# Gate GEMMs of a streaming encoder layer as block products of pairs, with the later jobs moved into the sliding-window stage and the rotation moved to VectorE

## The chip, the cores and the metric

The kernel runs on one NeuronCore of one Trainium2 chip. The metric is the device time of one execution in microseconds (us). The engines are TensorE (PE), VectorE (DVE), ScalarE (ACT), GpSimd (POOL) and SyncE (SP, here a DMA queue). All arithmetic is fp32. A product of two fp32 matrices is made of three passes: each operand is split into a high part that TensorE takes exactly (`hi`, written by ACT) and the rest (`lo`, written by DVE), and TensorE computes `lo*hi + hi*lo + hi*hi`.

## The reference, cut to what matters

One layer for 640 token rows (a prompt of 512 frames, and 8 streams of 16 new frames), model width 1024:

```
h      = rmsnorm(x) * g_pre_mix
z      = h @ w_in            # q latent 384 | kv latent 256 | rope key 32 | swa q 512, k 128, v 128 | gate logits 2048
q      = (rmsnorm(z_q) * g_q) @ w_uq,   ckv = rmsnorm(z_kv) * g_kv       # q's and k's last columns are rotated (rope)
o_mla  = latent attention, 8 heads, chunk-causal; the streams also read 128 cached frames
o_swa  = sliding window of 128 frames, 8 query and 2 key heads, with sinks
m      = sum_b sigmoid(gate_b) * (o_b @ w_branch[b])
x      = x + rmsnorm(m @ w_out)
x      = x + rmsnorm((silu(h2 @ w_gate) * (h2 @ w_up)) @ w_down),  h2 = rmsnorm(x) * g
```

The gate logits are a product of 640 x 1024 with 1024 x 2048. They are needed only when the branches are mixed, late in the kernel, and wait for it in a DRAM scratch.

## The kernel before, in words

The program is written out by hand: each engine has one instruction stream, and counting semaphores tie them. There is no planner. In order of time the stages are:

1. **Norm and input projection** (to 96.2 us): `tall` (L1207 on) makes the 1440 mixer columns of `z` in three chunks of 480 columns.
2. **First gates** (to 152.5): 8 slots of 128 gate columns. `wide` (L1184) runs 8 row blocks of the contraction by 2 token halves by 3 passes, 48 matmuls of 128x128 by 320 columns per slot. While it runs, ACT squares `z`, DVE normalises it, and POOL applies the rotation to all five token tiles at once (`rope_out`, L529 to L536), and then sends the new rows out (24 DMAs).
3. **Turns** (to 160.2): jobs of three kinds per token tile (`qlat`, `ckv`, `qs`) transpose `z` on PE; ACT and DVE copy the banks out.
4. **Query up-projection** (to 175.8): 10 jobs `uq`, each 9 matmuls of 384 columns.
5. **Sliding window** (to 253.9): 8 chunks of 64 frames. Per chunk PE makes `chunk_scores` (L1433), one gate slot with `chunk_values` of the previous chunk (L1458) in its middle, and `chunk_turn` (L1443). DVE takes the maximum (L1820), ACT the exponentials (L963), DVE divides (L1830), PE turns the result, ACT copies it (L973).
6. **Remaining jobs** (to 282.9): `kt` (keys from the latent), `q` (turning q), `cache` (turning the caches), `wuk`, `v`, `qabs`. They use four PSUM banks in turn, and PE waits with job j until job j-4 is copied out. The last `chunk_values` stands among them.
7. **Attention units**, then branches and mixing, output projection, the gate/up stage of the FFN, and the down projection.

A job's copies run on ACT where its number is odd and on DVE where it is even (`job_engine`). Every engine takes its instructions in order, so a copy that is written behind the exponentials of a chunk waits for them.

The FFN's gate/up stage of this kernel already works as block products of pairs: two weight columns of 128 and two token halves give a 2x2 block product over a contraction split in two, made with 7 products of 12 matmuls for 8. It is the same recipe that the change takes to the gates, so its rows serve below as measured prices of the new instructions: `L1952` a difference of two weight blocks on DVE, `L1036` a high part on ACT, `L1898` a low part on DVE, and 320-column reads of a bank (`L1095`, `L2018`).

Lines of the profile that the prediction uses: L1180 to L1182 (the three passes), L1306 `q`, L1310 to L1312 `cache`, L1317 `wuk`, L1328 `qabs`, L1332 `kt`, L1336 `v`, L802 (POOL clears `probs_m` behind a wait for all of `cv_done`).

## Time and profile before

| | before |
|---|---|
| median of 3 runs | 902.55 us (902.31 to 903.01) |
| the profiled execution's own time | 903.12 us |
| its span in the trace, granted TensorE clock | 901.3 us, 0.998 |
| PE, PEld busy | 885.1 us (98%), 804.0 us (89%) |
| DVE, ACT, POOL busy | 491.9, 385.4, 75.7 us |
| chain that ended last | PE 90%, DVE 5%, ACT 4%, issue 1% |
| matmuls, HBM traffic | 5513, 102 GB/s over the span |

The span runs from the first to the last instruction of the trace; 1.8 us of the execution lie around it. A row of busy time merges overlapping instructions: a 320-column matmul is shown with 309 ns, though one starts every 147 ns, because their ends overlap. The chain of waits shows the time that each piece adds.

### The profile page before, as it was taken

How to read it: one execution, taken by the hardware profiler on the slowest of the kernel's cores; microseconds unless marked ns; L12 is line 12 of the kernel's file. 1: busy time of each engine (PE TensorE's matmuls, PEld its weight loads, DVE VectorE, ACT ScalarE, POOL GpSimd, SP SyncE). 2: the span in 40 equal slices, each digit the busy share in tenths (PEclk: the TensorE clock that was granted, in tenths of full speed). 3: DMA queues.
4: the chain of work that ended last, by engine and by line, in shares of the span. 5: the costliest groups of instructions: out<-in, count | busy, mean ns of one | idle time of the engine just before them, and what ended most of it. 6: DMA issues, size and time to landing. Idle time of an engine off the chain costs nothing.

```text
span 901.3 us, 13817 instructions
## 1 busy us (share of the span) xinstructions
PE 885.1 (98%) x5513; PEld 804.0 (89%) x5513; DVE 491.9 (55%) x758; ACT 385.4 (43%) x769; POOL 75.7 (8%) x73
## 2 busy tenths in 40 slices
PE   8999999999999998999999999999999999999997
PEld 7888999999976877998789999999999998888886
DVE  5523532433354565564779877777777774343124
ACT  5211422335453555452666545444445443332112
POOL 0300197140030000000000000000000000000000
PEclk9999999999999999999999999999999999999999
DMA  7623245153330001654612233332233326222202
GB/s 271 176 78 93 69 128 179 57 158 92 100 71 1 2 1 36 205 181 181 193 72 81 83 93 95 94 87 76 73 94 94 94 84 242 72 72 93 71 24 117
DMA packets 101599, 91.97 MB, mean 102 GB/s; under 512 B 8496, under 2 KB 85312, under 8 KB 101392
## 3 DMA queue, kind: packets, MB, share of 16 engines
q1 hardware_dynamic: 95216, 86.19, 30.9%
q10 hardware_dynamic: 5424, 2.99, 1.1%
q0 software_dynamic: 896, 1.92, 0.7%
q8 instruction: 44, 0.72, 0.3%
q14 instruction: 19, 0.16, 0.1%
HBM read 79.60 MB, written 12.40 MB: 102 GB/s over the span
## 4 chain that ended last, share of the span: by engine, by line
PE 90%; DVE 5%; ACT 4%; issue 1%; DMA 0%; DVEq 0%; POOL 0%; ACTq 0%; POOLq 0%
PE ps L1180 26%; PE ps L1181 25%; PE ps L1182 25%; PE ps L1362 2%; PE ps L1411 1%; PE ps L1373 1%; PE ps L1235 1%; PE ps L1458 1%; PE ps L1332 1%; PE ps L1405 1%; PE ps L1336 1%; ACT probs L897 1%; PE ps L1433 1%; PE ps L1443 1%; DVE nm_c L1735 1%
## 5 line engine op out<-in xcount | busy, mean ns | idle before, releaser
L1671 DVE TENSOR_TENSOR wlo<-raw,whi 128x1024 fp32r<-128x1024 f32 x59 | 79.0, 1342 | 206.0 <-ACT whi L824 198.5
L824 ACT ACTIVATE whi<-raw 128x1024 fp32r<-128x1024 f32 x59 | 62.1, 1056 | 179.3 <-PE ps L1182 167.6
L1180 PE MATMUL ps<-h_hi,wlo 128*128 128x320 f32 x288 | 90.7, 315 | 0.0
L1182 PE MATMUL ps<-h_hi,whi 128*128 128x320 f32 x288 | 89.0, 309 | 0.0
L1181 PE MATMUL ps<-h_lo,whi 128*128 128x320 f32 x288 | 88.9, 309 | 0.0
L1180 PE MATMUL ps<-sc_hi,t_lo 128*128 128x320 f32 x252 | 77.9, 309 | 0.9 <-DVE t_lo L1898 0.9
L1036 ACT ACTIVATE t_hi<-wd 128x512 fp32r<-128x512 f32 x84 | 52.8, 629 | 60.3 <-DVE wd L1952 55.9
L1182 PE MATMUL ps<-sc_hi,t_hi 128*128 128x320 f32 x252 | 77.8, 309 | 0.0
L1181 PE MATMUL ps<-sc_lo,t_hi 128*128 128x320 f32 x252 | 77.8, 309 | 0.0
L1180 PE MATMUL ps<-whi,gu_lo 128*128 128x512 f32 x190 | 74.0, 390 | 0.2 <-DVE gu_lo L2022 0.2
L1181 PE MATMUL ps<-wlo,gu_hi 128*128 128x512 f32 x190 | 73.9, 389 | 0.0
L1182 PE MATMUL ps<-whi,gu_hi 128*128 128x512 f32 x190 | 73.9, 389 | 0.0
L1898 DVE TENSOR_TENSOR t_lo<-wd,t_hi 128x512 fp32r<-128x512 f32 x84 | 57.6, 686 | 2.0
L1180 PEld LDWEIGHTS ps<-h_hi,wlo 128*128 128x128 f32 x288 | 54.0, 188 | 2.8 <-issue 2.5
L1181 PEld LDWEIGHTS ps<-h_lo,whi 128*128 128x128 f32 x288 | 54.1, 188 | 0.0
L1182 PEld LDWEIGHTS ps<-h_hi,whi 128*128 128x128 f32 x288 | 54.1, 188 | 0.0
L1181 PE MATMUL ps<-h_lo,b_hi 128*128 128x320 f32 x168 | 51.8, 308 | 0.0
L1182 PE MATMUL ps<-h_hi,b_hi 128*128 128x320 f32 x168 | 51.7, 307 | 0.0
L1180 PE MATMUL ps<-h_hi,b_lo 128*128 128x320 f32 x168 | 51.5, 307 | 0.0
L1180 PEld LDWEIGHTS ps<-sc_hi,t_lo 128*128 128x128 f32 x252 | 47.3, 188 | 1.2 <-DVE t_lo L1898 1.2
L1182 PEld LDWEIGHTS ps<-sc_hi,t_hi 128*128 128x128 f32 x252 | 47.3, 188 | 0.0
L1181 PEld LDWEIGHTS ps<-sc_lo,t_hi 128*128 128x128 f32 x252 | 47.3, 188 | 0.0
(308 smaller groups left out, 2143.9 us busy)
## 6 DMA issues: line engine op xcount, KB each, us to landing
raw<-in_w_gate_up SPq DMA_DIRECT2D x44, 512.0 KB, 3.8
raw<-in_w_down SPq DMA_DIRECT2D x22, 512.0 KB, 3.7
raw<-in_w_in SPq DMA_DIRECT2D x16, 512.0 KB, 4.1
raw<-in_w_in SPq DMA_DIRECT2D x12, 480.0 KB, 4.8
gates_scratch<-gate_s SPq DMA_DIRECT2D x16, 320.0 KB, 2.4
gate_r<-gates_scratch SPq DMA_DIRECT2D x8, 640.0 KB, 4.4
raw<-in_w_branch SPq DMA_DIRECT2D x8, 512.0 KB, 5.3
raw<-in_w_out SPq DMA_DIRECT2D x8, 512.0 KB, 6.0
```

The lines of the kernel that those rows point to most:

```text
L824: act.activation(whi[:, r % 2, :] if to is None else to, raw[:, r, :], ACT.Copy).then_inc(w_hi, 1)
L897: act.activation((probs if of_prompt else probs_m)[:, 2 * slot + c, 0:nk], ps[:, b0 + c, 0:nk], ACT.Exp, bias=nm_c[:, col:col + 1], accum_ ...
L1036: act.activation(op_parts(kind, p)[0][:], op_source(kind, p), ACT.Copy).then_inc(op_hi_rdy, 1)
L1180: pe.matmul(out, left[1], right[0], start=first, stop=False, skip_group_check=not own_group)
L1181: pe.matmul(out, left[0], right[1], start=False, stop=False, skip_group_check=not own_group)
L1182: return pe.matmul(out, left[0], right[0], start=False, stop=last, skip_group_check=not own_group)
L1235: pe.transpose(ps[:, 7, 0:P], ident[:], ident[:])
L1332: ins = pe.matmul(bank[:, :], w_uk[:, ct, 2 * n:2 * n + 2, :], ckv_T[:, ct, 0:SEQ], start=(ct == 0), stop=(ct == 1))
L1336: ins = pe.matmul(bank[:, :], ckv_T[:, ct, c], w_uv[:, ct, :, :], start=(ct == 0), stop=(ct == 1))
L1362: ins = pe.matmul(out[:, 0:nk], q_T[:, h, a * P:(a + 1) * P], k_T[:, h, 0:nk], start=True, stop=True)
L1671: dve.tensor_tensor(lo[:, place, :], raw[:, r, :], hi[:, place, :].bitcast(F32), ALU.subtract).then_inc(w_lo, 1)
L1898: dve.tensor_tensor(lo[:], op_source(kind, p), hi[:].bitcast(F32), ALU.subtract).then_inc(op_lo_rdy, 1)
```

## The change

What it does:

- **Gates as one block of pairs.** The 16 gate columns become 8 pairs. Each pair takes 7 products of 12 matmuls (`gate_product`), 56 products in all, in one unbroken stage behind the input projection. Four of the seven weight operands of a pair are differences of blocks (`gate_difference`, DVE); ACT and DVE split each operand to hi and lo (512 columns each). Four sums of blocks of `h` are made once on DVE during the input projection (`h_add`, `hs_raw`, `part_sum_lo`; ACT `part_sum_hi`). ACT and DVE combine the products (`gate_read`), four reads on ACT and three on DVE per pair.
- **Rotation on VectorE.** `rope_products` (4 instructions) and `rope_sums` (6) of a token tile stand behind products 2, 7, ... and 4, 9, ... of the gate stage; `z_normalise` (10) behind products 13, 15, ... 31 and the key's rotation behind 34 and 36. The squares are on ACT behind products 1 to 10.
- **Jobs in the sliding-window stage.** `uq` 0 and 1 stay ahead of it; all other jobs stand inside the chunks (`CHUNK_JOBS`: a part between scores and the previous chunk's values, a part before the turn, a part behind it). They have two banks (`job_bank`), so PE waits with job j until job j-2 is copied out. Behind chunk 1, ACT and DVE split the two first branch weights. `chunk_values` of the last chunk is now the last of the stage.
- The loads of `w_ukv` move from ACT's queue at the start to SP's queue behind the gates; the cache loads wait for `uq` 8 and 9. POOL's rotation of q starts once `uq` 9 is copied out, and `cache` jobs wait for it.

The order of instructions on PE at the end of the sliding-window stage of the kernel before (`L1443` turn of the last chunk, `L1332` `kt`, `L1458` values, `L1306` `q`, `L1310` to `L1312` one `cache` job):

```order
L1443 MATMUL ps<-ident,probs_s 128x128 x8
L1332 MATMUL ps<-ckv_T,w_uk 128x512 x4
L1458 MATMUL ps<-pt_s,v_s 64x128 x8
L1332 MATMUL ps<-ckv_T,w_uk 128x512 x4
L1306 MATMUL ps<-ident,q_t 96x128 x40
L1310 MATMUL ps<-ident,c_ckv 128x128 x2
L1311 MATMUL ps<-ident,c_k 128x128
L1312 MATMUL ps<-ident,c_kpe 32x128
```

And on PE in chunk 4 of the changed kernel (`L1585` scores, `L1467` the four `wuk` jobs, `L1609` values of chunk 3, then the first of eight `cache` jobs; its turn, `L1596`, follows the eighth):

```order
L1585 MATMUL ps<-ks_T,qs_T 128x192 x4
L1467 MATMUL ps<-ident,w_uk 64x128 x16
L1609 MATMUL ps<-pt_s,v_s 64x128 x8
L1460 MATMUL ps<-ident,c_ckv 128x128 x2
L1461 MATMUL ps<-ident,c_k 128x128
L1462 MATMUL ps<-ident,c_kpe 32x128
```

The `cache`, `wuk` and `q` jobs stood one behind another with no softmax beside them; now they stand between the scores and the turn of a chunk. The last rows of that stage on PE in the changed kernel (`L1478` `qabs` 3, `L1488` `v` 2, the turn of chunk 7, `v` 3, its values):

```order
L1478 MATMUL ps<-q_Ts,wuk_T 128x128 x4
L1488 MATMUL ps<-w_uv,ckv_T 128x512 x2
L1596 MATMUL ps<-ident,probs_s 128x128 x8
L1488 MATMUL ps<-w_uv,ckv_T 128x512 x2
L1609 MATMUL ps<-pt_s,v_s 64x128 x8
```

In the kernel before, `kt`, `q` and the other jobs followed the values of chunk 7; now the attention units follow at once.

DVE in the gate stage of the kernel before (between the last copy of `z` and the first job):

```order
L1712 COPY z<-ps 128x480 x5
L1671 TENSOR_TENSOR wlo<-raw,whi 128x1024
L1723 RECIPROCAL r_z<-sd_z 128x5
L1726 SCALAR_TENSOR_TENSOR z<-z,r_z,gq_b 128x384 x5
L1723 RECIPROCAL r_z<-sd_z 128x5
L1726 SCALAR_TENSOR_TENSOR z<-z,r_z,gkv_b 128x256 x5
L1671 TENSOR_TENSOR wlo<-raw,whi 128x1024 x7
```

DVE around product 8 of the changed kernel (`L1938` and `L1934` reads of a bank, `L1917` a difference, `L1903` a low part, `L1956` and `L1957` the sums of the rotation of tile 1; its four products of 320 columns, `L1948`, stand just ahead):

```order
L1938 TENSOR_TENSOR g_out_102<-ps,g_u_0_98 128x320
L1917 TENSOR_TENSOR wd_g<-raw,wd_g 128x512
L1903 TENSOR_TENSOR g_m_lo<-raw,g_m_hi 128x512
L1903 TENSOR_TENSOR g_m_lo<-wd_g,g_m_hi 128x512
L1956 TENSOR_TENSOR z<-rope_a,rope_b 128x4x32
L1957 TENSOR_TENSOR z<-rope_c,rope_d 128x4x32
L1956 TENSOR_TENSOR z<-rope_a,rope_b 128x4x32
L1957 TENSOR_TENSOR z<-rope_c,rope_d 128x4x32
L1956 TENSOR_TENSOR z<-rope_a,rope_b 128x2x32
L1957 TENSOR_TENSOR z<-rope_c,rope_d 128x2x32
L1917 TENSOR_TENSOR wd_g<-raw 128x512
L1903 TENSOR_TENSOR g_m_lo<-raw,g_m_hi 128x512
```

Eight splits of 1024 columns have become 56 low parts and 32 differences of 512 columns, 24 reads, and the rotation between them.

The diff, cut to its core:

```diff
-JOBS = (
-    [(kind, t) for t in range(TILES) for kind in ("qlat", "ckv", "qs")]
-    + [("uq", n) for n in range(2 * TILES)]
-    + [("kt", n) for n in range(4)] + [("q", n) for n in range(2 * TILES)] + [("cache", b) for b in range(STREAMS)]
-    + [("wuk", n) for n in range(4)] + [("v", 0), ("v", 1)] + [("qabs", n) for n in range(4)] + [("v", 2), ("v", 3)]
-)
-JOBS1 = 5 * TILES
+TURNS = [(kind, t) for t in range(TILES) for kind in ("qlat", "ckv", "qs")]
+JOBS1 = len(TURNS)
+
+
+
+AHEAD = [("uq", 0), ("uq", 1)]
+CHUNK_JOBS = [
+    ([("uq", 2)], [("uq", 3), ("uq", 4)], []),
+    ([("uq", 5)], [("uq", 6), ("uq", 7)], []),
+    ([("uq", 8)], [("uq", 9), ("kt", 0)], []),
+    ([("kt", 1)], [("kt", 2), ("kt", 3)], []),
+    ([("wuk", n) for n in range(4)], [("cache", b) for b in range(STREAMS)], []),
+    ([("q", n) for n in range(4)], [("q", n) for n in range(4, 10)], []),
+    ([("v", 0)], [("v", 1), ("qabs", 0)], []),
+    ([("qabs", 1), ("qabs", 2)], [("qabs", 3), ("v", 2)], [("v", 3)]),
+]
+JOBS = TURNS + AHEAD + [job for chunk in CHUNK_JOBS for part in chunk for job in part]
...
-    return 4 + (j + 3) % 4 if j < JOBS1 else (j - JOBS1) % 4
+    return 4 + (j + 1) % 4 if j < JOBS1 else (j - JOBS1) % 2
...
+GATE_PAIRS = 8
+GATE_PRODUCTS = [("m1", 0), ("m2", 0)]
+for p in range(GATE_PAIRS - 1):
+    GATE_PRODUCTS += [("m5", p), ("m6", p), ("m1", p + 1), ("m7", p), ("m2", p + 1), ("m4", p), ("m3", p)]
+GATE_PRODUCTS += [(kind, GATE_PAIRS - 1) for kind in ("m5", "m6", "m7", "m4", "m3")]
+NG = len(GATE_PRODUCTS)
+GATE_BANKS = [(7, 0, 1), (2, 3, 4)]
...
+            def store_gates(p):
+                sp.wait_ge(g_c11, p + 1)
+                sp.wait_ge(g_c21, p + 1)
+                sp.dma_start(gates_dram[2 * p], g_out_s[p % 2][0][:]).then_inc(g_st[p % 2][0], 16)
+                sp.wait_ge(g_c22, p + 1)
+                sp.wait_ge(g_c12, p + 1)
+                sp.dma_start(gates_dram[2 * p + 1], g_out_s[p % 2][1][:]).then_inc(g_st[p % 2][1], 16)
...
+            sp.wait_ge(gp_used, NG)
+            for k in range(2):
+                sp.dma_start(w_uk[:, k], w_ukv[0, k * P:(k + 1) * P, :, 0:NOPE]).then_inc(wukv_in, 16)
+                sp.dma_start(w_uv[:, k], w_ukv[0, k * P:(k + 1) * P, :, NOPE:NOPE + VDIM]).then_inc(wukv_in, 16)
+            sp.dma_start(q_T[96:128], mask_q_dram.unsqueeze(1).to_broadcast([32, HEADS, SEQ])).then_inc(mask_in, 16)
+            sp.dma_start(k_T[96:128], mask_k_dram.unsqueeze(1).to_broadcast([32, HEADS, SEQ])).then_inc(mask_in, 16)
+            job_emptied(sp, job_index("uq", 8))
+            job_emptied(sp, job_index("uq", 9))
...
+            pool.wait_ge(gp_used, NG)
+            pool.tensor_copy(v_s[:], z[:, :, C_VS:MIX_COLS]).then_inc(v_s_rdy, 1)
+            job_emptied(pool, job_index("uq", 8))
+            job_emptied(pool, job_index("uq", 9))
...
+            def gate_split_hi(m):
+                kind, p = GATE_PRODUCTS[m]
+                if kind in DIFFERENCES:
+                    act.wait_ge(gp_diff, gate_difference_count(kind, p))
+                else:
+                    s = gate_slots(p)[kind == "m3"]
+                    act.wait_ge(w_raw[s % 4], 16 * (s // 4 + 1))
+                if p:
+                    act.wait_ge(gp_used, gate_count(kind, p - 1))
+                act.activation(gp_hi[kind][:], gate_source(kind, p), ACT.Copy).then_inc(gp_hi_rdy, 1)
...
+            for n in range(NG):
+                gate_read(n)
+                if n + LEAD + 1 < NG:
+                    gate_split_hi(n + LEAD + 1)
+                if 1 <= n <= 2 * TILES:
+                    z_square(n - 1)
...
+            def gate_product(n):
+                kind, p = GATE_PRODUCTS[n]
+                b_p, b_q, b_r = GATE_BANKS[p % 2]
+                bank = {"m2": b_q, "m5": b_r, "m3": b_r}.get(kind, b_p)
+                first = kind in ("m1", "m2", "m5")
+                left = {"m1": (0, 0), "m2": (4, 0), "m4": (4, HALF)}.get(kind)
+                i = {"m5": 0, "m6": 1, "m7": 2, "m3": 3}.get(kind)
+                pe.wait_ge(gp_lo_rdy, n + 1)
+                if kind == "m1":
+                    pe.wait_ge(g_c21, p - 1) if p >= 2 else pe.wait_ge(bank_empty, 10 + 5 * p)
+                elif kind == "m2" and p >= 2:
+                    pe.wait_ge(g_c11, p - 1)
+                elif kind == "m5" and p >= 2:
+                    pe.wait_ge(g_c12, p - 1)
+                elif kind == "m6":
+                    pe.wait_ge(g_u1_rdy, p + 1)
+                elif kind == "m7":
+                    pe.wait_ge(g_u2_rdy, p + 1)
+                elif kind == "m4":
+                    pe.wait_ge(g_u3_rdy, p + 1)
+                elif kind == "m3":
+                    pe.wait_ge(g_c22, p + 1)
+                if p == 0 and i is not None:
+                    pe.wait_ge(hs_lo_rdy, i + 1)
+                for k in range(4):
+                    w = slice(k * P, (k + 1) * P)
+                    if left is None:
+                        right = (hs_hi[:, i, k, :], hs_lo[:, i, k, :])
+                    else:
+                        cols = slice(left[1], left[1] + HALF)
+                        right = (h_hi[:, left[0] + k, cols], h_lo[:, left[0] + k, cols])
+                    ins = mm3(ps[:, bank, 0:HALF], (gp_hi[kind][:, w], gp_lo[kind][:, w]), right, first and k == 0, k == 3,
+                              first)
+                ins.then_inc(gp_used, 1)
...
+                elif j >= JOBS1 + 2:
+                    job_emptied(pe, j - 2)
...
             for c in range(NCH):
                 chunk_scores(c)
-                pe.wait_ge(w_lo, G1 + c + 1)
-                pe.wait_ge(g_out, 8 + c)
-                wide(c % 2, h_hi, h_lo, (0, 1), 0, 4, KD)
+                for j in chunk_jobs(c, 0):
+                    job(j)
                 if c:
                     chunk_values(c - 1)
-                wide(c % 2, h_hi, h_lo, (0, 1), 4, KD, KD).then_inc(w_used, 1)
+                for j in chunk_jobs(c, 1):
+                    job(j)
                 chunk_turn(c)
-            for j in range(JOBS1, len(JOBS)):
-
-                if j == JOBS1:
-                    pe.wait_ge(g_out, 16)
-                elif j == JOBS1 + 2:
-                    chunk_values(NCH - 1)
-                job(j)
+                for j in chunk_jobs(c, 2):
+                    job(j)
+            chunk_values(NCH - 1)
...
+            def h_add(half, part):
+
+                own = slice(4 * part, 4 * part + 4), slice(HALF * half, HALF * half + HALF)
+                dve.tensor_tensor(h_part[half, part][:], h_hi[:, own[0], own[1]].bitcast(F32),
+                                  h_lo[:, own[0], own[1]].bitcast(F32), ALU.add).then_inc(hs_part, 1)
+
+            def part_sum_lo(i):
+                dve.wait_ge(hs_hi_rdy, i + 1)
+                dve.tensor_tensor(hs_lo[:, i], hs_raw[:, i], hs_hi[:, i].bitcast(F32), ALU.subtract).then_inc(hs_lo_rdy, 1)
...
+            def gate_difference(kind, p):
+                gate, up = (s % 4 for s in gate_slots(p))
+                of = {"m5": (raw[:, up, 0:512], raw[:, gate, 0:512]),
+                      "m6": (raw[:, up, 512:1024], gate_source("m5", p)),
+                      "m7": (raw[:, up, 512:1024], raw[:, up, 0:512]),
+                      "m4": (raw[:, gate, 512:1024], gate_source("m6", p))}[kind]
+                if kind == "m5":
+                    for s in gate_slots(p):
+                        dve.wait_ge(w_raw[s % 4], 16 * (s // 4 + 1))
+                else:
+                    dve.wait_ge(gp_diff, gate_difference_count(kind, p) - 1)
+                dve.tensor_tensor(gate_source(kind, p), of[0], of[1], ALU.subtract).then_inc(gp_diff, 1)
+
...
+            def rope_products(t):
+                qk = z[:, t, C_QS:C_VS].rearrange("p (h d) -> p h d", d=HD)
+                cos_b = cos_t[:, t, :].unsqueeze(1).to_broadcast([P, 10, 32])
+                sin_b = sin_t[:, t, :].unsqueeze(1).to_broadcast([P, 10, 32])
+                if t:
+                    dve.wait_ge(z_rot, ROPE_STEPS * t)
+                for to, x, factor in ((rope_a, qk[:, :, 0:32], cos_b), (rope_b, qk[:, :, 32:64], sin_b),
+                                      (rope_c, qk[:, :, 32:64], cos_b), (rope_d, qk[:, :, 0:32], sin_b)):
+                    dve.tensor_tensor(to[:], x, factor, ALU.mult).then_inc(z_rot, 1)
+
+            def rope_sums(t):
+
+                pairs = z[:, t, C_QS:C_KS].rearrange("p (i g d) -> p i g d", i=4, g=2)
+                keys = z[:, t, C_KS:C_VS].rearrange("p (h d) -> p h d", d=HD)
+                dve.wait_ge(z_rot, ROPE_STEPS * t + 4)
+                for heads, to in ((slice(0, 4), pairs[:, :, 0, :]), (slice(4, 8), pairs[:, :, 1, :]), (slice(8, 10), keys)):
+                    dve.tensor_tensor(to[:, :, 0:32], rope_a[:, heads], rope_b[:, heads], ALU.subtract).then_inc(z_rot, 1)
+                    dve.tensor_tensor(to[:, :, 32:64], rope_c[:, heads], rope_d[:, heads], ALU.add).then_inc(z_rot, 1)
...
+            for n in range(NG):
+                gate_read(n)
+                if n + LEAD + 1 < NG and GATE_PRODUCTS[n + LEAD + 1][0] in DIFFERENCES:
+                    gate_difference(*GATE_PRODUCTS[n + LEAD + 1])
+                if n + LEAD < NG:
+                    gate_split_lo(n + LEAD)
+                if n < 5 * TILES and n % 5 == 2:
+                    rope_products(n // 5)
+                elif n < 5 * TILES and n % 5 == 4:
+                    rope_sums(n // 5)
+                if 13 <= n < 13 + 4 * TILES and n % 2:
+                    z_normalise((n - 13) // 2)
+                elif n == 34:
+                    key_rope_products()
+                elif n == 36:
+                    key_rope_sums()
...
+                for j in chunk_jobs(c, 0):
+                    job(j)
                 chunk_normalise(c)
                 if c:
                     chunk_out(c - 1)
-                after_slot(G1, 0, c)
+                for part in (1, 2):
+                    for j in chunk_jobs(c, part):
+                        job(j)
+                if c == 1:
+                    split_lo(BRC + 1, 0)
+                    split_lo(BRC + 2, 1)
```

## Rows read from the trace of the kernel before

**Rows 1.** Windows: us, then PE, PEld, DVE, ACT, POOL busy (x), clock, DMA share, GB/s

```profile
50.00:100.00 50.00, 50.00 (x241) 43.86 (x240) 16.61 (x18) 10.88 (x17) 0.72 (x1) 1.00 0.28 73
...
96.20:152.50 56.30, 56.30 (x385) 56.28 (x384) 19.64 (x22) 18.52 (x37) 43.65 (x43) 1.00 0.47 133
152.50:160.23 7.73, 7.39 (x58) 5.90 (x57) 5.84 (x17) 4.40 (x9) 0.85 (x1) 1.00 0.15 61
160.23:175.84 15.61, 15.61 (x93) 15.36 (x91) 5.93 (x16) 4.11 (x7) 0.00 (x0) 1.00 0.06 22
175.84:253.85 78.01, 78.01 (x601) 72.48 (x601) 26.66 (x38) 35.74 (x103) 14.00 (x12) 1.00 0.39 113
253.85:282.93 29.08, 29.08 (x171) 19.86 (x171) 15.50 (x29) 13.69 (x30) 9.17 (x10) 1.00 0.24 56
```

**Rows 2.** Timeline of the FFN's gate/up stage: start, us, instruction [idle before <-releaser]

```profile
602.13 0.49 DVE L2018 TENSOR_TENSOR gu_f<-c,u 128x320 f32<-128x320 f32 x1
602.54 0.69 DVE L1952 TENSOR_TENSOR wd<-raw,wd 128x512 f32<-128x512 f32 x1
603.14 0.68 DVE L1898 TENSOR_TENSOR b_lo<-raw,b_hi 128x512 fp32r<-128x512 f32 x1
603.26 0.64 ACT L1036 ACTIVATE t_hi<-wd 128x512 fp32r<-128x512 f32 x1 [2.53 <-DVE wd L1952]
...
605.06 0.44 ACT L1095 ACTIVATE u<-ps 128x320 f32<-128x320 f32 x1 [0.64 <-PE ps L1182]
```

**Rows 3.** Timeline of DVE, first gate stage: the normalising

```profile
103.95 2.74 DVE L1726 SCALAR_TENSOR_TENSOR z<-z,r_z,gq_b 128x384 f32<-128x384 f32 x5
```

**Rows 4.** Timeline of ACT around chunk 6 of the sliding window

```profile
234.26 1.08 ACT L973 ACTIVATE pt_s<-ps 128x512 f32<-128x512 f32 x2
...
236.52 0.42 ACT L963 ACTIVATE probs_s<-ps,nm_c 128x193 f32<-128x193 f32 x1 [1.19 <-DVE nm_c L1820]
```

**Rows 5.** The same chunk's rows of DVE

```profile
235.53 0.95 DVE L1820 TENSOR_REDUCE nm_c<-ps 128x4 f32<-128x772 f32 x1
238.28 0.18 DVE L1828 RECIPROCAL inv_c<-sum_c 128x4 f32<-128x4 f32 x1 [1.79 <-ACT probs_s L963]
238.49 0.96 DVE L1830 TENSOR_TENSOR probs_s<-probs_s,inv_c 128x768 f32<-128x768 f32 x1
```

**Rows 6.** Costliest groups: splits of a 1024-column slot, busy us, mean ns

```profile
L1671 DVE TENSOR_TENSOR wlo<-raw,whi 128x1024 fp32r<-128x1024 f32 x59 | 79.0, 1342 | 206.0 <-ACT whi L824 198.5
L824 ACT ACTIVATE whi<-raw 128x1024 fp32r<-128x1024 f32 x59 | 62.1, 1056 | 179.3 <-PE ps L1182 167.6
```

**Rows 7.** Chain of waits, last chunk and the jobs behind it: start, us, piece

```profile
243.67 0.85 PE ps L1433 x8
...
252.98 0.87 PE ps L1443 x8
253.85 3.68 PE ps L1332 x8
257.54 1.02 PE ps L1458 x16
...
262.19 4.55 PE ps L1306 x40
...
270.23 1.87 PE ps L1317 x16
...
275.54 3.77 PE ps L1328 x32
```

**Rows 8.** Timeline of DVE: copies of a `q` job and of a `cache` job

```profile
265.47 0.69 DVE L1784 TENSOR_SCALAR q_T<-ps 96x512 f32<-96x512 f32 x1 [0.19 <-PE ps L1306]
...
269.11 0.42 DVE L1786 COPY ckv_Ta<-ps 128x256 f32<-128x256 f32 x1
...
269.75 0.28 DVE L1786 COPY kpe_Ta<-ps 32x128 f32<-32x128 f32 x1
```

**Rows 9.** Timeline of POOL, end of the jobs stage

```profile
259.50 0.95 POOL L802 MEMSET probs_m<- 128x1024 f32 x1
```

435 lines of the change are left out of this document (271 added, 164 removed).

## The prediction

> **What bounds the kernel now.** I read three views. The windows by stage come first [rows 1]: from 96.2 us to 282.9 us PE is busy for 186.4 of 186.7 us at clock 1.00, while DVE has 73.6 and ACT 76.5 (sums over the last five rows). So in the whole stretch that the change rewrites PE is the bound, and what PE issues less is gained in full, as long as nobody makes it wait. The chain of waits [rows 7] confirms it: the pieces follow each other without a gap and carry PE's name. The timelines [rows 2 to 5, 8] then give prices of what DVE and ACT must do between two PE pieces, which decides whether PE stays unbroken. Before, every softmax chunk had a gate slot of 7 us as cover; that cover is what the change spends.
>
> **What PE saves.** The first gate window has 384 matmuls in 56.3 us, 147 ns each [rows 1]. Both gate stages are 768 matmuls (112.6 us); 56 products of 12 are 672 (98.5 us): 14.1 us less. A second, smaller gain: the sliding-window window takes 78.0 us [rows 1]; its gate slots are 56.3, and scores, turns and values at 0.85, 0.87 and 1.02 us [rows 7], with the two first, shorter chunks at about two thirds, come to 18.7. The 3.0 us left I put down to the change between softmax pieces and gate matmuls, some fifteen times 0.2; only `uq` jobs keep such changes, five of them, so 2.0 us go. The turns (7.7 us), `uq` (15.6) and the other jobs (29.1) stay as they are. PE's own work falls from 186.7 to 170.6 us.
>
> **What is hidden.** DVE makes twelve block sums or parts of `h` of 1280 columns in the input projection, 1.7 us each by the 1.34 us for 1024 [rows 6], some 20 us over 40; DVE is busy for 16.6 of 50 us there [rows 1] and the pieces stand between splits that have to wait anyway. I cost it at nothing; were it late, PE would wait for the weights of the projection. POOL's work behind the gates is 14.0 + 9.2 us [rows 1]; it starts when `uq` 9 is copied, with some 50 us left: nothing. The 24 stores on POOL's queue start behind product 36, 20 products before the end, and the loads of weights have the same pattern as in the FFN's stage, which shows no wait for them: nothing.
>
> **What DVE costs in the gate stage.** Per pair 11 instructions of 512 columns and 3 of 320. Start to start these take 0.60 us (602.54 to 603.14) and 0.41 us (602.13 to 602.54) [rows 2], so 1.12 us per product against PE's 1.76. The rotation of a tile is 4 instructions of 320 columns (1.64), and 6 of 128 and 64 columns, which the trace of before does not show. The step from 512 to 320 is 1 ns a column, which gives 0.22 and 0.15; with the wait for the products of 0.1 a tile costs 2.9 us. The bounds of a 128-column piece are 0.15 (as a 64-column one) and 0.29 (the whole 0.49 of a 320-column row less the columns), 2.6 to 3.3 us a tile. I take 2.9, by the row nearest to it. A normalising instruction is 0.55 for 384 columns [rows 3], 0.42 estimated for 256. DVE comes to product 1 at about 101.1 us, since the last copies of `z` and five splits stand ahead. To the end of product 25's share that is 25 x 1.12 + 5 x 2.9 + 4.1 (seven normalising, two reciprocals) = 46.6 us, so 147.7; PE would end product 25 at 141.9. What bites is not the low part, which has a lead of five products, but ACT's order: the read behind product 26, for which product 28 waits, stands behind a high part that waits for DVE's difference of that same share. Difference done at 146.8, high part 0.64, read 0.44 [rows 2]: 147.9, where product 28 would start at 145.4. That is 2.5 us, and with the hand-overs between I take 3.0. From product 33 on DVE has only its 1.12 per product and catches up, which gives nothing back. The last pair has no other pair's products between: m7 and m4 each wait for a read of 0.44 plus hand-over, 1.0 us together.
>
> One rule of the Trainium skill speaks against the price per instruction. On DVE two rows of 0.69 and 0.68 us stand 0.60 apart [rows 2]. The page VectorE: DVE Perf Modes, section The DRAIN you can't avoid, says that the next operation does not start before the pipe is empty; by that the distance would be the full length of a row. The trace of the FFN does not bear this out for independent instructions. What it would give is a rival below.
>
> **What two banks and the missing cover cost in the window stage.** I walk each chunk from its first score. A softmax takes scores 0.85, maximum 0.95, exponentials 1.76 (236.52 to DVE's 238.28), division 1.17, so PE can turn 4.8 us after the first score [rows 4, 5]; PE has 5.3 us and more of its own to do from the first score to the turn in every chunk, so alone this costs nothing. Four places do cost:
> - Chunk 2. ACT first copies chunk 1's turn (0.7), then two splits of 1.06; DVE's low parts (1.34 each [rows 6]) stand ahead of its maximum and end at 4.5, the maximum at 5.4, exponentials 7.2, division 8.3. PE's own work to the turn is 0.85 + 1.56 + 0.59 + 1.56 + 1.84 = 6.4: 1.9 us.
> - Chunk 4. `wuk` 3 needs the bank of `wuk` 1, whose copy on ACT stands behind the exponentials: 4.2 instead of 2.3. After the values (5.7) come eight `cache` jobs of 0.44 (266.74 to 270.23 [rows 7]), each with 0.92 of copies [rows 8]. With four banks the copies of the two engines overlapped PE's work; with two, a pair costs 0.44 + 0.92 + hand-overs, 1.5 us instead of 0.9. The turn can start at 11.4, own work is 7.2: 4.2 us.
> - Chunk 5. The same with ten `q` jobs (0.46 each [rows 7], copies 0.69 [rows 8]): turn at 9.5, own work 6.4: 3.1 us.
> - Chunk 7. `qabs` 3 waits for `qabs` 1 behind the exponentials: 0.5 us.
> At the end the values of chunk 7 have nothing behind them: POOL's 0.95 us for `probs_m` [rows 9], which waits for them, is now in PE's way, as are the two copies of the output: 1.1 us.
>
> **The sum.** 3.0 + 1.0 + 1.9 + 4.2 + 3.1 + 0.5 + 1.1 = 14.8 us of waits against 16.1 saved. 186.7 becomes 185.4. The profiled execution took 903.12 us (span 901.3 and 1.8 around it); less 1.3 is 901.8, and as that execution lies 0.57 above the median of the runs, 901.3 us.
>
> **The rivals.**
> - *DVE is the bound of the gate stage.* If an instruction holds DVE for its full row (0.69, 0.49, and 0.29 and 0.22 for the short ones), a product costs 1.29 and a tile 3.7 us; DVE ends product 25's share at 155.9 and product 28 starts 10.4 us late, 7.4 more: 909 us. It decides from where the five tiles and 25 products cost DVE more than 44 us. For it: each rotation starts with a wait on DVE's own last result, and strided halves of heads have no row here. Against it: 0.60 and 0.41 in the FFN. The skill's rule named above leads here. Slower. 0.20.
> - *The engines keep up better than my walk.* ACT's reads or short pieces of the rotation are cheaper and DVE has slack left, so that the gate stage flows (3.0) and chunk 2's splits fit in (1.9): 896.4, about 897 us. For it: each wait was worked out with hand-overs that the chain shows at only some 0.04 us. 0.20.
> - *Nothing waits*, and the full 16.1 us are gained: 886.5 us. Two banks against a copy of 0.92 speak against it. 0.04.
> - *A transfer is late.* The cache loads go out when `uq` 9 is copied, some 15 us before the first `cache` job; before, they had 78 us, so the trace does not bound their wait from above; `w_ukv` has some 28 us. At 5 us of waiting 906 us. 0.06.
>
> **How the numbers follow.** This kernel's measurement tells 0.2%, 1.8 us, from no change: faster is below 900.75, slower above 904.35. My forecast (0.50) spans 899 to 904.5, since each of the five larger waits may be off by a third: 0.15 of it is faster, 0.33 the same, 0.02 slower. Faster: 0.15 + 0.20 + 0.04 = 0.39. Same: 0.33. Slower: 0.20 + 0.06 + 0.02 = 0.28. The range 895 to 908 holds the forecast, the faster rival, the late transfer and the nearer half of DVE's rival (3.3 us a tile and some longer starts); left out are its far end and the full gain.
>
> **What would show it.** The gate stage from first to last of its matmuls lasts about 102.5 us, with PE whole for twenty products, gaps ahead of m4 of pairs 2 and 3 released by ACT's read `g_u3`, and two gaps of half a microsecond at the end. In the window stage PE waits at `kt` 0 and the turn of chunk 2, in the middle of `wuk`, between pairs of `cache` and `q` jobs, released by ACT's and DVE's copies, and hardly in chunks 0, 1, 3 and 6. Matmuls fall by 96. The forecast is wrong if PE waits from product 8 on at every m4 (DVE's rival), if it waits at the first `cache` job for a DMA, or if the input projection no longer ends at 96.2.

## The result, and the profile after

| kernel | median, us | executions | ratio to before (95% interval) |
|---|---|---|---|
| before | 902.50 | 6 (902.05 to 903.01) | |
| changed | 906.09 | 6 (904.20 to 907.10) | 1.0036 (1.0023 to 1.0049) |
| changed, second measurement, beside 27 executions of before (median 902.32) | 905.74 | 5 (905.03 to 907.49) | 1.0036 (1.0022 to 1.0050) |

The change makes the kernel slower by 0.36%, 3.6 us. The forecast was 901.3 us, with the kernel before and the changed one nearly level. The profiled execution of the changed kernel is its fastest, 904.20 us (span 902.4), so there are two things to explain: 2.9 us between forecast and that execution, and some 1.8 more in most of the others.

The page's line of busy times, and then windows of the changed kernel (us from the start, then PE, PEld, DVE, ACT, POOL busy, clock, DMA share, GB/s):

```profile
PE 873.0 (97%) x5417; PEld 787.8 (87%) x5417; DVE 561.4 (62%) x922; ACT 406.5 (45%) x829; POOL 45.4 (5%) x57
```

```profile
95.23:199.07 103.84, 99.71 (x674) 98.53 (x672) 82.37 (x177) 47.10 (x107) 12.52 (x24) 1.00 0.48 145
...
95.23:209.97 114.74, 110.21 (x747) 107.26 (x745) 91.16 (x205) 52.11 (x117) 13.23 (x25) 1.00 0.53 153
209.97:283.71 73.74, 64.83 (x457) 47.59 (x457) 36.61 (x65) 40.74 (x123) 21.67 (x18) 1.00 0.13 36
```

The 96 matmuls are gone (5513 to 5417 on PE). From the first gate matmul to the first of attention, the kernel before takes 186.56 us (96.21 to 282.77, PE busy for 186.22 of them); the changed one takes 114.74 + 73.74 = 188.48, and PE is busy for 175.04. So PE has 11 us less to do and waits 13 more. From the first attention matmul to the start of the last matmul of the kernel it is 612.61 us in the trace of before and 612.72 in that of the changed kernel. The start differs from execution to execution, not by the change: over the thirteen profiles of the changed kernel and its variants the gate stage begins between 94.86 and 96.24 us, and the 44 transposes that open the program take 6.4 to 7.9.

Every wait of the gate stage, in PE's timeline (start, us, instruction, [idle before <- who ended it]; `g_m_lo` is the low part of a weight operand, `g_u` a bank read by ACT):

```profile
134.09 0.38 PE L1293 MATMUL ps<-h_hi,g_m_lo 128*128 128x320 f32 x1 [1.38 <-ACT g_u L982]
...
148.05 0.38 PE L1293 MATMUL ps<-h_hi,g_m_lo 128*128 128x320 f32 x1 [1.40 <-ACT g_u L982]
...
192.86 0.39 PE L1293 MATMUL ps<-hs_hi,g_m_lo 128*128 128x320 f32 x1 [0.62 <-ACT g_u L978]
...
195.48 0.38 PE L1293 MATMUL ps<-h_hi,g_m_lo 128*128 128x320 f32 x1 [0.62 <-ACT g_u L982]
```

These are the m4 of pairs 2 and 3 and the last pair's m7 and m4, where the prediction put them. ACT's rows ahead of the first show the order that bites: the read `g_u` (L982) stands behind a high part that waited 2.38 us for DVE's difference.

```profile
132.99 0.63 ACT L964 ACTIVATE g_m_hi<-wd_g 128x512 fp32r<-128x512 f32 x1 [2.38 <-DVE wd_g L1917]
133.53 0.42 ACT L982 ACTIVATE g_u<-ps 128x320 f32<-128x320 f32 x1
```

DVE's timeline gives the prices of the short pieces for which [rows 2] had to stand in, read from start to start:

```profile
106.60 0.28 DVE L1956 TENSOR_TENSOR z<-rope_a,rope_b 128x128 f32<-128x128 f32 x1
106.80 0.28 DVE L1957 TENSOR_TENSOR z<-rope_c,rope_d 128x128 f32<-128x128 f32 x1
...
107.41 0.22 DVE L1956 TENSOR_TENSOR z<-rope_a,rope_b 128x64 f32<-128x64 f32 x1
107.54 0.22 DVE L1957 TENSOR_TENSOR z<-rope_c,rope_d 128x64 f32<-128x64 f32 x1
...
111.15 0.48 DVE L1948 TENSOR_TENSOR rope_a<-z,cos_t 128x320 f32<-128x320 f32 x1
111.55 0.48 DVE L1948 TENSOR_TENSOR rope_b<-z,sin_t 128x320 f32<-128x320 f32 x1
```

0.20 us for 128 columns, 0.13 for 64, 0.40 for 320: a tile costs 4 x 0.40 + 1.15 = 2.75 us (forecast 2.9). A full row each would set the two 128-column rows 0.28 apart; they are 0.20 apart. So the drain that the Trainium skill describes (VectorE: DVE Perf Modes, section The DRAIN you can't avoid) does not space these instructions; what the same section says of an operation that is not held, that it starts earlier, agrees with this 0.20.

The window stage, chunks 4 and 5, PE's rows with a wait (`L1467` is `wuk`, `L1460` `cache`, `L1455` `q`):

```profile
242.62 0.63 PE L1467 MATMUL ps<-ident,w_uk 128*64 128x128 f32 x4 [0.66 <-DVE wuk_T L2069]
244.25 0.63 PE L1467 MATMUL ps<-ident,w_uk 128*64 128x128 f32 x4 [1.00 <-ACT wuk_T L1061]
...
247.68 0.44 PE L1460 MATMUL ps<-ident,c_ckv 128*128 128x128 f32 x2 [0.75 <-DVE kpe_Ta L2069]
...
249.34 0.44 PE L1460 MATMUL ps<-ident,c_ckv 128*128 128x128 f32 x2 [0.57 <-DVE kpe_Ta L2069]
...
251.01 0.44 PE L1460 MATMUL ps<-ident,c_ckv 128*128 128x128 f32 x2 [0.57 <-DVE kpe_Ta L2069]
...
255.48 0.64 PE L1455 MATMUL ps<-ident,q_t 128*96 128x128 f32 x4 [0.65 <-DVE q_T L2067]
257.11 0.64 PE L1455 MATMUL ps<-ident,q_t 128*96 128x128 f32 x4 [0.99 <-ACT q_T L1061]
...
260.32 1.08 PE L1455 MATMUL ps<-ident,q_t 128*96 128x128 f32 x8 [0.53 <-DVE q_T L2067]
261.74 1.08 PE L1455 MATMUL ps<-ident,q_t 128*96 128x128 f32 x8 [0.34 <-DVE q_T L2067]
```

In the kernel before, the same jobs ran at four banks without a gap: `q` 4.55, `wuk` 1.87 us [rows 7], and the eight `cache` jobs 3.51, from the first of these rows of before to the second:

```profile
266.58 0.38 PE L1310 MATMUL ps<-ident,c_ckv 128*128 128x128 f32 x2
270.09 2.01 PE L1317 MATMUL ps<-ident,w_uk 128*64 128x128 f32 x16
```

In the changed kernel they take 6.10 us (245.84 to 251.94), of which the three rows above count 1.89 as idle. Chunk 2 waits at `kt` 0 and at its turn, `qabs` 3 waits 0.50, and attention begins behind POOL's clearing:

```profile
228.23 1.98 PE L1484 MATMUL ps<-ckv_T,w_uk 128*128 128x512 f32 x4 [0.46 <-DVE q_t L2069]
230.73 1.09 PE L1596 MATMUL ps<-ident,probs_s 128*128 128x128 f32 x8 [0.51 <-DVE probs_s L2113]
...
283.71 0.73 PE L1510 MATMUL ps<-ckv_Ta,qabs 128*128 128x144 f32 x4 [1.37 <-POOL probs_m L874]
```

### The profile page after: what moved, and what is told of

Same layout as the page of the kernel before. It is cut to its first block, busy times and chain, and to the rows that moved or that the text cites. A ratio compares the mean times of both kernels' runs of the same rounds, so it can differ in the third digit from the quotient of the medians.

```text
span 902.4 us, 13913 instructions
## 1 busy us (share of the span) xinstructions
PE 873.0 (97%) x5417; PEld 787.8 (87%) x5417; DVE 561.4 (62%) x922; ACT 406.5 (45%) x829; POOL 45.4 (5%) x57
## 3 DMA queue, kind: packets, MB, share of 16 engines
q0 software_dynamic: 896, 1.92, 0.6%
## 4 chain that ended last, share of the span: by engine, by line
PE 83%; DVE 8%; ACT 5%; DMA 2%; issue 1%; POOL 0%; SPq 0%; DVEq 0%; ACTq 0%; POOLq 0%
PE ps L1293 24%; PE ps L1294 24%; PE ps L1295 24%; PE ps L1514 2%; PE ps L1563 1%; PE ps L1525 1%; DMA raw<-in_w_out 1%; PE ps L1488 1%; PE ps L1557 1%; ACT probs_s L1075 1%; PE ps L1596 1%; ACT probs L1026 1%; DMA raw<-in_w_in 1%; DVE wlo L1818 1%; DVE nm_c L2018 1%
## 5 line engine op out<-in xcount | busy, mean ns | idle before, releaser
L1818 DVE TENSOR_TENSOR wlo<-raw,whi 128x1024 fp32r<-128x1024 f32 x43 | 52.4, 1224 | 119.7 <-ACT whi L896 112.2
L896 ACT ACTIVATE whi<-raw 128x1024 fp32r<-128x1024 f32 x43 | 45.2, 1059 | 162.3 <-PE ps L1295 160.1
L2182 DVE TENSOR_TENSOR b_lo<-raw,b_hi 128x512 fp32r<-128x512 f32 x63 | 43.1, 685 | 0.0
L1293 PEld LDWEIGHTS ps<-whi,gu_lo 128*128 128x128 f32 x190 | 35.7, 188 | 8.0 <-DVE gu_lo L2306 0.6
L964 ACT ACTIVATE g_m_hi<-wd_g 128x512 fp32r<-128x512 f32 x32 | 20.2, 630 | 49.1 <-DVE wd_g L1917 47.8
L1294 PEld LDWEIGHTS ps<-wlo,gu_hi 128*128 128x128 f32 x190 | 35.7, 188 | 7.4
L1295 PEld LDWEIGHTS ps<-whi,gu_hi 128*128 128x128 f32 x190 | 35.7, 188 | 7.3
L1293 PE MATMUL ps<-hs_hi,g_m_lo 128*128 128x320 f32 x128 | 39.6, 309 | 0.6 <-ACT g_u L978 0.6
```

The source lines that it names most:

```text
L896: act.activation(whi[:, r % 2, :] if to is None else to, raw[:, r, :], ACT.Copy).then_inc(w_hi, 1)
L964: act.activation(gp_hi[kind][:], gate_source(kind, p), ACT.Copy).then_inc(gp_hi_rdy, 1)
L1293: pe.matmul(out, left[1], right[0], start=first, stop=False, skip_group_check=not own_group)
L1294: pe.matmul(out, left[0], right[1], start=False, stop=False, skip_group_check=not own_group)
L1295: return pe.matmul(out, left[0], right[0], start=False, stop=last, skip_group_check=not own_group)
L1818: dve.tensor_tensor(lo[:, place, :], raw[:, r, :], hi[:, place, :].bitcast(F32), ALU.subtract).then_inc(w_lo, 1)
```

## The experiments

All were timed against the kernel before, in several executions each; "changed" is the kernel with the change, and "below the changed kernel" is counted from its second measurement, 905.74 us. That one stands beside g1_rope, s1_splits and w1_order; for the later experiments the kernel before had medians of 902.37 to 902.75 instead of 902.32, so their distance from the changed kernel is uncertain by some 0.5 us. Lengths of a stretch are read from one profiled execution each. The stretch named in them runs from the first gate matmul to attention, the window stage from the first window scores to attention.

**a0_again: the changed kernel, unaltered.** 

> The changed kernel once more, unaltered, timed against the kernel before. Its profiled execution took 904.2 us, five others 904.4 to 907.1, while six of the kernel before lay within 1.0 us. Theory 1 (waits of two engines that nearly tie, so the losses differ between executions; or a start that differs): median 905 to 906.5 again, about 0.3 to 0.4% above the kernel before, and a spread of 2 to 3 us. If the profiled execution is one of the slow ones, some stretch of its trace is longer than in the first trace, and that says where: in the start (0 to 95 us) if it is the start, in the gate stage (103.8 us long in the first trace) or the window stage (73.7 us from the first window scores to attention) if it is the new stages, after 290 us if it is neither. Rival: the first measurement was off and the median is within 0.2% of before.

Measured: 905.74 us. The first measurement was right, so the rival falls. The numbers of theory 1 hold, its causes do not: the profiled execution (906.06 us) has the same stretch to 0.01 us, 188.49, and starts it 0.22 us later. The rest of what it has more lies behind the stretch, in attention: 1.63 us from the first attention matmul to the last matmul. Windows of this execution, and then of the first one:

```profile
347.00:349.00 2.00, 1.75 (x10) 1.33 (x11) 0.97 (x2) 0.90 (x5) 0.00 (x0) 0.55 0.00 0
349.00:351.00 2.00, 2.00 (x10) 1.46 (x10) 0.58 (x1) 0.00 (x0) 0.00 (x0) 0.59 0.00 0
```

```profile
347.00:349.00 2.00, 1.98 (x16) 1.59 (x16) 0.96 (x3) 0.67 (x4) 0.00 (x0) 1.00 0.00 0
349.00:351.00 2.00, 1.49 (x12) 0.92 (x10) 1.70 (x6) 1.50 (x6) 0.00 (x0) 1.00 0.00 0
```

The third number from the right is the granted clock. For 3.4 us it is at 0.50 of full speed (1.2 of 2.4 GHz), and the same instructions take some 1.6 us longer. Ahead of the fall PE had waited 1.12, 0.21 and 0.45 us between short pieces; the execution without a fall has the same waits to 0.01 us.

The record of each execution has its mean granted clock. Of the eleven executions of the changed kernel in both measurements, five have a mean of 0.996 and took 905.74 to 907.49 us (on average 906.5), and six have 0.998 or 0.999 and took 904.20 to 906.48 (905.3). All 27 of the kernel before have 0.998 or more. The mean does not say where a fall lay: the end of most traces, where PE has no work left, is at half clock too, 2 to 3 us of it in the kernel before.

**g1_rope: rotation and normalising spread in DVE's order.** 

> Only VectorE's order in the gate stage changes: rotation of a tile every eighth product instead of every fifth, normalising every third instead of every second, the narrow keys at products 42 and 44. Same instructions. Theory 1 (VectorE's queue is late where rotation and normalising lie close together, which costs the two m4 waits of 1.4 us with their PEld idle): both waits go, gate stage 103.8 -> 100.8 to 101.3 us, time 2.5 to 3 us below the changed kernel (0.3%). Rival (the two waits come from ScalarE's own order, which reads bank u3 after the next splits): both waits stay and the time is within 0.5 us. Second rival: the stores of z go out 14 us later and the first up-projection waits for them: the gain is given back in one wait at the end of the turns.

```
-                if n < 5 * TILES and n % 5 == 2:          # sums: n % 5 == 4
+                if n < 8 * TILES and n % 8 == 2:          # sums: n % 8 == 5
-                if 13 <= n < 13 + 4 * TILES and n % 2:
+                if 13 <= n < 13 + 6 * TILES and n % 3 == 1:
```

Measured: 902.84 us (11 executions, 900.83 to 903.90), 2.9 below the changed kernel; ratio to before 1.0002 (0.9993 to 1.0011). Both m4 waits are gone, nothing new waits, and gates plus turns fall from 114.74 to

```profile
95.04:206.54 111.50, 109.73 (x746) 107.27 (x744) 90.87 (x205) 52.66 (x117) 13.24 (x25) 1.00 0.53 156
```

Theory 1 holds, and gives a second number: the waits were 1.38 + 1.40 = 2.78 us of idle time, and the stretch is 3.24 shorter. Each wait costs 0.23 us more than its row says, because the row counts only from the end of the matmul before, which is drawn 0.16 us into its follower (0.31 us long, the next one 0.15 later), and the matmul behind a wait is followed after 0.22 us (134.09 to 134.31) instead of 0.15.

**s1_splits: the branch-weight splits out of chunk 1.** 

> Only the two branch-weight splits move: ScalarE's and VectorE's halves from the end of chunk 1 to chunks 5 to 7 (ScalarE's behind its copies of the turned probabilities of chunks 5 and 6, VectorE's behind the maxima of chunks 6 and 7). Theory 1: the waits of chunk 2 (0.46 at the first key up-projection, 0.51 ahead of its turn) go, and chunks 6 and 7 hide the splits: time 1 to 1.9 us below the changed kernel. Rival: VectorE meets the splits again in chunks 6 and 7 and the turns there wait as long: same time within 0.4 us, with the wait moved.

```
 ACT   -  if c == 1: split_hi(0, ...); split_hi(1, ...)        # behind chunk_pt(c)
       +  if c in (5, 6): split_hi(c - 5, ...)
 DVE   -  if c == 1: split_lo(BRC + 1, 0); split_lo(BRC + 2, 1)
       +  if c in (6, 7): split_lo(BRC + c - 5, c - 6)         # behind chunk_max(c)
```

Measured: 903.77 us, 2.0 below. The window stage is 72.36 us long, 1.38 less, for two rows with 0.97 us of idle time together: 0.2 more for each wait again. Theory 1 holds.

**w1_order: the list of window jobs, first form.** 

> Only the list of jobs in the window stage changes: the query transposes, the w_uk transposes and the key up-projection alternate and stand at most two in a row, so that each copy out of a bank has another job or a part of a chunk beside it; the four cache jobs stay together. Theory 1 (with two banks, a transpose job of 0.9 us followed by its like waits for the copy before last, 0.5 to 1.0 us each): the waits between query jobs (0.65, 0.99, 0.53, 0.34) and at w_uk (0.66, 1.00) go, those between the cache jobs (three of 0.6) stay; stage 73.7 -> about 69.5 us, time 4 us below the changed kernel. Rival (what is lost is not these waits but the switch of TensorE between kinds of work, some 0.2 to 0.3 us each, of which this order has more): gain under 1.5 us, and the rows of busy PE become longer where waits go.

The list is shown shortened, from chunk 2 on: `uq 8` stands for `("uq", 8)`, `cache 0..7` for all eight.

```
-    ([uq 8], [uq 9, kt 0], []),              ([kt 1], [kt 2, kt 3], []),
-    ([wuk 0..3], [cache 0..7], []),          ([q 0..3], [q 4..9], []),
-    ([v 0], [v 1, qabs 0], []),              ([qabs 1, qabs 2], [qabs 3, v 2], [v 3])
+    ([uq 8], [uq 9, wuk 0], [wuk 1]),        ([kt 0], [wuk 2, kt 1], [wuk 3, kt 2]),
+    ([kt 3, q 0], [cache 0..7], [q 1]),      ([q 2, q 3], [v 0, q 4], [q 5, q 6]),
+    ([v 1, q 7], [q 8, q 9], []),            ([qabs 0, qabs 1], [qabs 2, qabs 3], [v 2, v 3])
```

(There are eight cache jobs, not four as the expectation says.) Measured: 902.62 us, 3.1 below. The waits between `q` jobs and between `wuk` jobs are gone. Chunk 2's first wait of 0.46 now stands ahead of `wuk` 0, its turn waits 1.87 us, and while the cache jobs waited (1.07, 0.60, 0.16 and 0.30 us), the clock fell:

```profile
250.00:253.00 3.00, 2.84 (x14) 2.17 (x13) 1.00 (x4) 0.82 (x3) 2.36 (x1) 0.50 0.00 0
```

The window stage is 71.16 us with that fall, an estimated 69.5 without it (less the 1.6 us that the fall cost in a0_again). Theory 1 holds, but this list can do better.

**w3_order: the list, second form, and nothing else.** 

> The changed kernel with only the list of window jobs altered, now with the eight cache jobs (0.5 us of TensorE each, copies of 1.0 us) set apart too, one or two beside a key or value up-projection of 1.8 us or a part of a chunk. The first reordering left the eight together: scores of chunk 0 to attention went from 73.7 to 71.2 us, with a clock fall of 1.7 us inside it. Theory 1 (waits with two banks, and each wait costs 0.2 us more than its idle row): the waits of the cache jobs go as well, this stretch is 68.5 to 69 us, and TensorE, never idle long, keeps its clock there: time 5 to 5.5 us below the changed kernel, 900.3 to 901. Rival (the copies are the bound: eight of 1.0 us and ten of 0.6 to 0.7 us beside the chunks' own work on two engines): waits move to the turns, stretch 71 us, time 902.5 as before.

```
+    ([uq 8], [uq 9, kt 0], [wuk 0]),         ([kt 2], [wuk 1, kt 1], [wuk 2]),
+    ([q 0, kt 3, cache 0], [cache 1, cache 2], [q 1, wuk 3]),
+    ([q 2, v 0, cache 3], [cache 4, q 3], [cache 5, q 4]),
+    ([cache 6, v 1, q 5], [q 6, q 7], [cache 7, q 8]),
+    ([v 2, q 9], [qabs 0, qabs 1], [qabs 2, qabs 3, v 3])
```

(With it, attention waits for `qabs` 3 too.) Measured: 897.44 us (897.11 to 898.00), 8.3 below the changed kernel, 0.9944 (0.9930 to 0.9958) of before. The window stage:

```profile
209.73:276.18 66.45, 63.78 (x457) 47.74 (x457) 35.73 (x65) 40.47 (x123) 21.69 (x18) 1.00 0.15 41
```

7.29 us less than 73.74, with the same two banks, the same 457 matmuls and the same copies. From chunk 3 to attention one wait of 0.17 us is left, and the one ahead of attention. DVE and ACT, which copy, are busy for 36 and 40 of the 66 us; it was the neighbourhood of like jobs that cost. The gain was larger than expected, and the rival falls. It is smaller, though, than the waits that went: those of chunks 4, 5 and 7 count 6.56 us of idle time in ten rows, 8.9 us with 0.23 for each. PE pays for the alternation: a cache job set apart takes 0.44 to 0.53 us where eight in a row took 0.44 each.

**t1_tail: two transpose jobs among the last products.** 

> The changed kernel with two of the transpose jobs (latent and cache columns of token tile 0) put on TensorE between the last products of the gate block: one ahead of the last pair's m4, one ahead of its m3. Theory 1: the two waits of 0.62 us there are covered by transposes that come anyway; gate stage and turns together 1.0 to 1.3 us shorter, time about 1 us below the changed kernel. Rival (each change of kind of work costs TensorE 0.2 to 0.3 us, and there are four more of them): gain under 0.4 us.

```
+            for n in range(NG):
...
+                if n >= NG - 2:
+                    job(n - NG + 2)
+                gate_product(n)
+            for j in range(2, JOBS1 + len(AHEAD)):
```

Measured: 905.15 us (903.80 to 905.73). In the trace gates and turns take 114.61 us instead of 114.74; of two waits of 0.62 one became 0.29, and a new one of 0.24 stands ahead of job 3. By the trace the rival holds: filling a wait of 0.6 with a 0.3 us piece of another kind gives next to nothing. The median is 0.6 us below the changed kernel all the same, which the two intervals against before (1.0019 to 1.0039, 1.0022 to 1.0050) do not tell from nothing.

**e1_end: the last job behind the last values.** 

> The changed kernel with its last job (value up-projection of tile 3) on TensorE behind the values of chunk 7 instead of ahead of them; ScalarE copies the chunk's output ahead of that job. Theory 1: GpSimd's clearing of probs_m, which waits for those values, now lies beside the job: the 1.37 us wait ahead of attention falls to 0.3 to 0.5 us, time 0.9 us below the changed kernel. Rival: the values of chunk 7 now wait for the copies of its probabilities, which the job had covered: same time within 0.3 us.

```
 PE    chunk_values(NCH - 1)
       +  job(len(JOBS) - 1)         # no longer ahead of it; ACT: behind chunk_out(NCH - 1)
```

Measured: 904.82 us (903.80 to 907.19). From the last scores to attention it is 12.18 us instead of 12.28. POOL's clearing is covered, and the rival's wait is there in its place:

```profile
283.77 1.09 PE L1611 MATMUL ps<-pt_s,v_s 128*64 128x128 f32 x16 [1.18 <-ACT pt_s L1085]
```

Alone it gives 0.1 us by the trace; the profiled execution had two falls of the clock (246 to 249 and 259 to 263 us), which makes its total no measure. The median of nine is 0.9 below the changed kernel, the number of theory 1. Its interval (1.0018 to 1.0038) overlaps that of the changed kernel, and the trace shows why theory 1's reason does not hold, so the 0.9 stays unexplained.

**d1_delay: 1 us of transposes ahead of the turns.** 

> The changed kernel with nine more transposes of the identity (about 1.0 us at 0.11 us each) on TensorE ahead of the first transpose job; their output is not used. They shift everything behind them in time and change nothing else. In a profiled execution of the changed kernel of 906.1 us, the granted clock was 0.55 to 0.59 from 347 to 351 us, in one of 904.2 us it was 1.00 there; the stretch took 1.65 us more. Theory P (whether the clock falls in attention's thin part hangs on when that part is reached): the share of executions with the fall changes, and the median is not 1.0 us above the changed kernel but up to 2 us away from that, on either side. Theory Q (the fall comes from waits in the window stage before, however late): the median is 1.0 us above the changed kernel, 906.8 to 907, with the same spread.

```
+            for n in range(9):
+                pe.transpose(ps[:, 5, 0:P], ident[:], ident[:])
```

Measured: 905.38 us (six executions, 904.66 to 906.01), no fall in the profile, and a stretch 1.00 us longer. With 1 us more work the kernel is no slower. That its executions had fewer falls is inferred, and their mean granted clocks bear it out: 0.998 or 1.0 in all six, where five of eleven of the changed kernel have 0.996. This speaks against theory Q. But theory P does not hold as put either: w1_order and s1_splits reach attention at 282.09 and 282.14 us, and only the first had the fall at 345.

**all1: the mends together, with a third list of jobs.** 

> The changed kernel with all four mends: VectorE's rotation spread over forty products; two transpose jobs between the last products; the branch-weight splits in chunks 5 to 7; the jobs of the window stage alternating (key up-projection in the order 0, 2, 1, 3, the last w_uk job and query job 0 ahead of the cache jobs); the last job behind the values of chunk 7. Theory 1 (the waits add up, each at its own place): 3 + 1 + 1.5 + 3.5 + 0.9 = 10 us below the changed kernel, 896 us, 0.7% below the kernel before. Rival (TensorE, once whole, is held by something else: the stores of z, the loads of the cache, GpSimd's rotation of the queries): 899 to 901, with one new wait of over 1 us at the first up-projection, the first cache job or the first query job.

Its list keeps the cache jobs together: chunk 2 `([uq 8], [uq 9, kt 0], [wuk 0])`, chunk 3 `([kt 2], [wuk 1, kt 1], [wuk 2, kt 3])`, chunk 4 `([q 0, wuk 3], [cache 0..7], [q 1])`, the rest as in w1_order. Measured: 896.85 us (0.9932; 0.9918 to 0.9945), within 1 us of the expected sum, and in none of the rival's places is there a wait: theory 1 holds. With `v` 2 ahead of the last values and `v` 3 behind them, neither the values nor attention waits. The cache jobs wait 0.61, 1.24, 0.57 and 0.16 us, and the clock falls there (245 to 249 us).

**b1_bank: cache job 1 in a third bank.** 

> The kernel with all mends (896.85 us) with cache job 1 in a third bank, number 6, which lies idle between the output of chunk 2 and the values of chunk 4, and without the transpose jobs among the last gate products (alone those had shortened gates and turns by only 0.13 us). In the trace of the kernel with all mends the cache jobs waited 0.61, 1.24, 0.57 and 0.16 us, and the granted clock was 0.5 from 246 to 249 us, which costs 1.5 to 1.7 us more. Theory 1: the waits of 1.24 and 0.57 fall to 0.2 or less, 1.5 to 2 us; and TensorE, idle less there, keeps its clock, another 1.7 us in those executions that had the fall: 893.5 to 895. Rival (VectorE's and ScalarE's copies of 1.3 us are the bound, not the banks): the wait moves to the last cache job and query job 1, gain under 0.6 us, fall as before.

```
+        elif (kind, i) == ("cache", 1):
+            out.append(6)            # PE waits for co_lo >= 3; values of chunk 4 wait for its copy
```

Measured: 894.28 us (4 executions, 893.71 to 894.93). The stretch is 178.94 us against all1's 179.42, and the wait of 1.24 and the fall (245 to 248) are still there: DVE has the division and the chunk's output ahead of its first cache copy (rows at 241.19, 242.06 and 242.40 us), and no bank helps with that. The trace gives 0.5 us, as the rival said. The median is 2.6 lower and lies where theory 1 put it. The mean granted clocks differ: three of the five executions of all1 have 0.993 and took 896.85 to 897.23, the other two 894.51 and 895.58; here three of four have 0.998 or 0.999. So most of the 2 us go with the clock; whether the bank is why, four and five executions do not show.

**all2: the same with three transpose jobs among the last products.** 

> As the last one (third bank), and with three transpose jobs among the last gate products: two ahead of the last m7, one ahead of the last m4, where TensorE waited 0.62 us each. Theory 1: a wait of 0.62 us costs 0.23 more in the pipeline's tail and start, so covering both with 0.76 and 0.44 us of transposes saves 0.8 to 1.2 us beside the last one. Rival (switching kind costs as much as the wait): within 0.3 us of the last one.

Measured: 893.86 us (893.01 to 895.57), a median 0.4 from the last. Gates and turns take 110.96 us against 111.47 in b1_bank: 0.5 us, between the two theories. One wait of 0.18 is left of the two of 0.62, and one of 0.68 stands ahead of job 3, which waits for the last read of a gate bank.

**all3: all mends, with w3_order's list and two banks.** 

> All mends with this list of jobs, three transpose jobs among the last gate products, no third bank. Gate start to attention was 179.4 and 177.3 us in the kernels with the cache jobs together. TensorE's own work in this stretch, from what was forecast before the change was timed, is 170.6 us. Theory 1: no wait of over 0.5 us is left in the window stage: 175 to 176 us for the stretch, 891.5 to 892.5 us in all, and executions differ by less because no fall of the clock starts there. Rival (copies are the bound): 893.5 to 894.5, as the last one, with waits of 0.5 us or more ahead of the turns of chunks 4 to 6.

Measured: 891.44 us (890.98 to 893.55), 0.9885 (0.9870 to 0.9900) of before, the fastest kernel of this study. Two windows of its stretch:

```profile
94.86:205.81 110.95, 109.64 (x746) 107.23 (x744) 90.83 (x205) 52.55 (x117) 13.24 (x25) 1.00 0.53 157
205.81:270.57 64.76, 63.50 (x457) 47.84 (x457) 36.93 (x65) 40.09 (x122) 21.83 (x19) 1.00 0.17 45
```

175.71 us, 10.85 less than the kernel before and 12.77 less than the changed one, with waits of 2.16 us in six rows. The length is the one of theory 1. A wait of over 0.5 us is left in the window stage all the same, 0.79 ahead of a `q` job at 253.92 us, and one execution took 893.55.

## Why the prediction was wrong

The places and causes of the waits were right; the sum was not. In the table, "idle rows" adds the idle time that the trace of the changed kernel shows at each place, with the number of waits, and the next column adds 0.23 us for each of them. All in us:

| term | forecast | idle rows | rows + 0.23 each | recovered by |
|---|---|---|---|---|
| m4 of pairs 2 and 3 | 3.0 | 2.78 (2) | 3.24 | g1_rope: 3.24 |
| last pair | 1.0 | 1.24 (2) | 1.70 | t1_tail: 0.13 |
| chunk 2 | 1.9 | 0.97 (2) | 1.43 | s1_splits: 1.38 |
| chunk 4 | 4.2 | 3.55 (5) | 4.70 | w3_order: 7.29 for chunks 4, 5 and 7 |
| chunk 5 | 3.1 | 2.51 (4) | 3.43 | |
| chunk 7, `qabs` 3 | 0.5 | 0.50 (1) | 0.73 | |
| end of stage | 1.1 | 1.37 (1) | 1.60 | e1_end: 0.1 alone; no wait left in all1 |
| sum | 14.8 | 12.92 | 16.8 | |

- **The step that failed first is the price of the waits.** The seven terms were worked out as walks over start times, with small hand-overs. With 0.23 us in each of seventeen waits for the pipeline's end and restart, 3.9 us in all, they cost 16.8, not 14.8; the last pair (1.70 for 1.0), chunk 4 and the end of the stage (0.5 each) miss by most. Two experiments measured the price (0.23 and 0.20), and the `cache` jobs give it once more without one: 6.10 us less the unbroken 3.51 and the idle 1.89 leaves 0.70 for three waits. For the other waits it is carried over from these.
- **PE's own work fell by less.** 188.48 - 16.8 leaves 171.7 us, where 170.6 was forecast: 14.9 saved of 186.56, not 16.1. The matmuls' 14.1 is certain (96 at 147 ns); the term of 2.0 for fewer changes between kinds of work, an estimate from a remainder, was at most 0.8. The rows show it directly. From start to start the gate slots in the window stage of before take 58.5 us, 2.2 above their 56.3 and not 3.0; and less their waits, the eight `uq` jobs, the `v` and the `qabs` jobs of the changed window stage take some 0.8, 0.4 and 0.3 us more than in before, because each now follows another kind of work.
- Together that turns the stretch's forecast of -1.3 us into +1.9. The forecast itself had left only a chance of 0.02 for a slower kernel; the other 0.26 for slower stood with DVE as the bound and with a late transfer, and neither came. The loss came by the forecast's own mechanism, with its terms too small. The start was 1.0 us lucky in the first profiled execution, so its 904.2 hides a part: 903.12 + 1.92 - 0.98 is 904.1.
- **The clock was in no term.** The prediction took the clock as 1.00 throughout, as the rows of before show it. The second trace of the changed kernel (a0_again) shows a fall that costs 1.6 us, and eleven executions of it lie between 904.2 and 907.5, where the largest set of before, 27 executions, spans 1.7 us (901.78 to 903.47). The executions with a mean clock of 0.996 are on average 1.2 us longer than the others. Falls and an ordinary start are the likely way from 904.2 to the median of 906; how large each share is was not separated.
- **DVE's rival (909 us) falls**: DVE's instructions start closer than their rows are long (0.60, 0.40, 0.20 and 0.13 us apart; a tile of the rotation costs 2.75 us, where 2.9 was forecast and 3.7 was the rival's), PE waits at products 21 and 28 and not from product 8 on. That DVE was busy for most of the first half did matter, but only through the order on ACT, and g1_rope removes both waits without removing an instruction. The faster rivals fall: chunk 2's splits did not fit, and every wait of the walk was there. No transfer was late: neither the first `cache` job nor the first `uq` waits.
- **What was hidden stayed hidden.** The block sums of `h` cost nothing: the gate stage begins at 95.2 us in the first trace and nowhere later than 96.24. Chunks 0, 1, 3 and 6 show no wait.
- **The end**: the forecast blamed POOL's clearing. e1_end shows two locks on the same 1.4 us: with the job moved, the values wait for their probabilities' copy. In all1, with a job of 1.8 us on either side of the values, neither wait is left.

**What stays open** is why the clock falls in some executions. Falls of 3 to 4 us at 0.5 while PE had work were seen in six of thirteen profiles of the changed kernel and its variants, either where PE waits between short transposes (245 to 263 us) or in attention's thin part (339 to 351 us), and not in the one profile of before. all3 shows none and still has one execution 2 us above the others, with a mean clock of 0.998 like two of those. w3_order has the fall in attention with no wait of over 0.2 us in chunks 3 to 7, so those waits are not its cause. The Trainium skill (TensorE: Matmul & The Clock Gate, section A second HAM failure mode: psum-queue depth-cycling) describes, for a bf16 kernel, a clock that oscillates when PE idles briefly and often while it cycles through banks. The falls at the cache jobs of w1_order, all1 and b1_bank, behind waits of 1.07, 1.24 and 1.24 us, agree with it; the first profile of the changed kernel and that of all2 have such waits too (0.75 and 1.24 us at the cache jobs) and no fall. Which execution is hit, no run here shows.

## What to carry to other kernels

When work that had served as cover is taken off the bounding engine, count how many waits the rest will have, not only how long they are: here each cost about 0.23 us beyond its idle time, and in some executions the clock fell among short waits. Before adding banks or thinning out an engine, reorder: with two banks, the third of a row of jobs whose copies took longer than the jobs had to wait; alternating them with long matmul jobs gave back 7.3 of the 73.7 us, though a short job set apart cost up to 0.1 us more. A filler of half the length of a wait gained nothing that the trace can tell (0.13 us in t1_tail).

## What the runs showed of the hardware

In the traces of the changed kernel, independent DVE instructions of two fp32 operands start 0.60, 0.40, 0.20 and 0.13 us apart for 512, 320, 128 and 64 columns, though their rows last 0.68, 0.48, 0.28 and 0.22 us. A wait on PE that the profile shows as 1.38 us of idle time lengthens the kernel by some 0.23 us more. And the granted clock of PE can drop to half for 3 to 4 us within one execution of a kernel and not in the next, at the same instructions and the same waits before them.
